# Value and output projections of a hybrid decoder layer: the 64-token tile with its low parts stacked beside its high parts

## The reference

```python
cb, cc, ch, q, k, v, g, a_lr, ga, gb = jnp.split(xn @ w_in, splits, axis=-1)   # xn = rmsnorm(x)
y_a = (cb * z) @ w_conv_out                     # z = short_conv(cc * ch)
o, S = gla(q, k, v, log_a, gla_state)           # gated linear attention, 4 heads
y_b = (rmsnorm(o) * silu(g)) @ w_gla_out
m = sigmoid(ga) * y_a + sigmoid(gb) * y_b
h = x + m @ w_o
h = h + hmoe(rmsnorm(h))                        # 32 experts, top-1 group, top-2 experts
y = rmsnorm(h)
```

## Time and profile before

| | us |
|---|---|
| median of 3 runs | 922.8 |
| lowest, highest | 921.0, 928.88 |
| the profiled execution | 922.86 |
| its span, from the first to the last instruction | 920.7 |

### The profile page before, as it was taken

One profiled execution on the slowest core, in us unless ns is written; L12 is line 12 of the kernel. 1 busy time (PEld: TensorE's weight loads), 2 busy tenths in 40 slices (PEclk: granted clock), 3 DMA queues, 4 the chain that ended last, 5 costly groups with the idle time before them and its releaser, 6 DMA issues.

```text
span 920.7 us, 12589 instructions
## 1 busy us (share of the span) xinstructions
PE 795.8 (86%) x5330; PEld 645.3 (70%) x5330; DVE 293.6 (32%) x507; ACT 237.6 (26%) x347; POOL 79.2 (9%) x121
## 2 busy tenths in 40 slices
PE   3899979999999999999999989965899788788740
PEld 3899979999988899999989989962333333233210
DVE  5420340566435362111464533243100000000007
ACT  5422432254411124422231211220221111111102
POOL 3000000001012210000000000111011100100003
PEclk9799989999999999999999989975999989988975
DMA  7412121111325642122215173179899999999726
GB/s 200 142 46 91 55 83 46 46 47 46 115 93 167 199 137 93 53 86 92 92 46 195 46 265 125 43 287 383 334 412 410 409 410 409 408 407 407 307 101 226
DMA packets 82147, 173.99 MB, mean 189 GB/s; under 512 B 10946, under 2 KB 49346, under 8 KB 81524
## 3 DMA queue, kind: packets, MB, share of 16 engines
q1 hardware_dynamic: 75108, 155.22, 46.1%
q0 software_dynamic: 6992, 18.10, 5.3%
HBM read 162.77 MB, written 17.86 MB: 196 GB/s over the span
## 4 chain that ended last, share of the span: by engine, by line
PE 74%; DMA 12%; DVE 5%; SPq 4%; ACT 3%; issue 2%; POOL 1%; POOLq 0%; ACTq 0%; DVEq 0%
PE ps L1535 52%; PE ps L1826 9%; DMA wgu<-w_up 9%; SPq L396 3%; PE ps L1843 3%; PE ps L1625 1%; DMA xin<-x_sample 1%; PE ps L1818 1%; PE ps L1683 1%; DMA xg<-moe_rows,slots 1%; PE ps L1672 1%; PE ps L1764 1%; PE ps L1639 1%; PE ps L1637 1%; PE ps L1636 1%
## 5 line engine op out<-in xcount | busy, mean ns | idle before, releaser
L1535 PE MATMUL ps<-xh,wh 128*128 128x288 f32 x832 | 181.6, 300 | 3.9 <-ACT hist L792 2.0
L1535 PE MATMUL ps<-xh,wl 128*128 128x288 f32 x832 | 179.4, 297 | 0.0
L1535 PE MATMUL ps<-xl,wh 128*128 128x288 f32 x832 | 179.2, 297 | 0.0
L1826 PE MATMUL ps<-wgu,gx 128*64 128x512 f32 x512 | 130.4, 668 | 27.5 <-DMA wgu<-w_up 26.4
L999 DVE TENSOR_TENSOR wl<-raw,wh 128x2048 fp32r<-128x2048 f32 x36 | 82.5, 2292 | 201.8 <-ACT wh L701 201.7
L1535 PEld LDWEIGHTS ps<-xh,wh 128*128 128x128 f32 x832 | 135.1, 190 | 7.7 <-issue 5.2
L1535 PEld LDWEIGHTS ps<-xh,wl 128*128 128x128 f32 x832 | 135.2, 190 | 0.0
L1535 PEld LDWEIGHTS ps<-xl,wh 128*128 128x128 f32 x832 | 134.9, 190 | 0.0
L1826 PEld LDWEIGHTS ps<-wgu,gx 128*64 128x64 f32 x512 | 44.1, 153 | 112.3 <-issue 110.8
L701 ACT CAST wh<-raw 128x2048 fp32r<-128x2048 f32 x36 | 68.6, 1905 | 61.0 <-PE ps L1535 59.6
L1479 DVE TENSOR_TENSOR hm<-si,ps 128x256 f32<-128x256 f32 x16 | 6.7, 421 | 227.7 <-ACT si L934 227.7
(11 more groups left out here) (296 smaller groups left out, 945.6 us busy)
## 6 DMA issues: line engine op xcount, KB each, us to landing
wgu<-w_gate SPq DMA_DIRECT2D x32, 1024.0 KB, 14.5
wgu<-w_up SPq DMA_DIRECT2D x32, 1024.0 KB, 20.3
wd<-w_down SPq DMA_DIRECT2D x32, 1024.0 KB, 20.2
raw<-w_in SPq DMA_DIRECT2D x26, 1024.0 KB, 5.3
raw<-w_gla_out SPq DMA_DIRECT2D x4, 1024.0 KB, 5.1
raw<-w_o SPq DMA_DIRECT2D x4, 1024.0 KB, 5.4
y<-moe_results SPq DMA_DIRECT2D x4, 1024.0 KB, 7.9
xin<-x_prompt SPq DMA_DIRECT2D x4, 512.0 KB, 6.5
```

Source lines behind the costliest of these rows:

```text
L1535: last.append(mm(out, left(a, k), right(b, k, o), start=k == 0 and n == 0, stop=k == k_tiles - 1 and n == 2))
L1826: ins = mm(ps[half * B:(half + 1) * B, bank, :].rearrange("t (n c) -> t n c", n=2), x[:, k, half * B:(half + 1) * B], w[half][:, :, :].rea ...
```

## The change

For the 64-token tile alone, the three passes become two. The 64 unused columns T to TP of `xh` and `mh` now hold the low parts of the 64 tokens. The stationary operand `[high | low]` (128 columns) is multiplied with `wh`: rows 0 to 63 of the PSUM region get high x high, rows 64 to 127 low x high. The second pass multiplies the 64 high columns with `wl` and adds to rows 0 to 63. So there are 16 matmuls in the place of 24, and the two halves of the region are added behind.

```diff
             def token_unit(p, u, t, x, ks=range(KD)):
                 w = (tiles(wh[p], KD), tiles(wl[p], KD))
+                if t == NPT:
+                    for k in ks:
+                        mm(ps[:, 2 * u, 0:256], x[0][:, k, SEQ:TP], w[0][:, k, :], start=k == 0, stop=False,
+                           skip_group_check=True)
+                        ins = mm(ps[0:ND, 2 * u, 0:256], x[0][:, k, SEQ:T], w[1][:, k, :], start=False, stop=k == KD - 1,
+                                 skip_group_check=True)
+                    return ins
```

```diff
             for i in range(NT):
                 rms(i, i, i + 1, D)
+            pool.wait_ge(unit_free[1], N_G // 2)
+            pool.tensor_tensor(v[0:ND, NPT, :], v[0:ND, NPT, :], vlo[:, :], ALU.add).then_inc(vd_ready, 1)
...
-                    copy(v[:, t, k * 256:(k + 1) * 256], ps[:, 2 * u, 0:256]).then_inc(unit_free[u], 1)
+                    if t == NPT:
+                        c(copy(v[0:ND, t, cols], ps[0:ND, 2 * u, 0:256]))
+                        copy(vlo[:, cols], ps[ND:P, 2 * u, 0:256]).then_inc(unit_free[u], 1)
...
-                    tt(hv, hv, ps[:, 2 * u, 0:256], ALU.add).then_inc(h_ready, 1)
+                    if t == NPT:
+                        hv = h[0:ND, t, k * 256:(k + 1) * 256]
+                        c(tt(hv, hv, ps[0:ND, 2 * u, 0:256], ALU.add))
+                        c.sync()
+                        tt(hv, hv, ps[ND:P, 2 * u, 0:256], ALU.add).then_inc(h_ready, 1)
```

```diff
-                tt(xl[:, :, i * P:(i + 1) * P], ps[...], xh[...], ALU.subtract).then_inc(xt_free, 1)
+                n = ND if i == NPT else P
+                if i == NPT:
+                    c(tt(xh[:, :, T:TP], x, high, ALU.subtract))
+                tt(xl[:, :, i * P:i * P + n], x, high, ALU.subtract).then_inc(xt_free, 1)
...
-            c(dve.memset(mh[:, :, T:TP].bitcast(F32), 0.0))
-            c(dve.memset(ml[:, :, T:TP].bitcast(F32), 0.0))
-            c.sync()
...
                         dve.wait_ge(m_hi, k * 2 + (u + 1))
+                        tt(mh[:, one, T:TP].rearrange("p a t -> p (a t)"), tmp[u][:, SEQ:T],
+                           mh[:, one, SEQ:T].rearrange("p a t -> p (a t)").bitcast(F32), ALU.subtract)
                         tt(ml[:, one, 0:T]..., ALU.subtract).then_inc(m_ready, 1)
```

More of the change, by code:

```diff
@@ L196, in build @@
         mnt = sb("mnt", [P, T])
+        vlo = sb("vlo", [ND, D], at=zone_q - 4 * D)
         m_tile = sb("m_tile", [P, H, P], at=s1)
@@ L328, in build @@
         st_store, km_ready, dkv_full, st_ready = (sem(n) for n in ("st_store", "km_ready", "dkv_full", "st_ready"))
-        pair_const = sem("pair_const")
+        vd_ready = sem("vd_ready")
         cc_ready, z_mul, z_hi, z_ready, cs_ready, cs_full, cso_ready = (
@@ L712, in high_of_x @@
                 b = TB + 2 * (i % 2)
-                copy(xh[:, :, i * P:(i + 1) * P], ps[:, b:b + 2, :].rearrange("p a (c t) -> p (a c) t", t=P)
+                n = ND if i == NPT else P
+                copy(xh[:, :, i * P:i * P + n], ps[:, b:b + 2, :].rearrange("p a (c t) -> p (a c) t", t=P)[:, :, 0:n]
                      ).then_inc(xh_ready, 1)
@@ L786, in _ @@
                     wait_unit(act, k + G_V, k, t, NT, U_V)
-                    copy(v[:, t, k * 256:(k + 1) * 256], ps[:, 2 * u, 0:256]).then_inc(unit_free[u], 1)
+                    cols = slice(k * 256, (k + 1) * 256)
+                    if t == NPT:
+                        c(copy(v[0:ND, t, cols], ps[0:ND, 2 * u, 0:256]))
+                        copy(vlo[:, cols], ps[ND:P, 2 * u, 0:256]).then_inc(unit_free[u], 1)
+                    else:
+                        copy(v[:, t, cols], ps[:, 2 * u, 0:256]).then_inc(unit_free[u], 1)
                 high(k % 2, (G_V + k) // 2 + 1)
@@ L1007, in low_of_x @@
                 b = TB + 2 * (i % 2)
-                tt(xl[:, :, i * P:(i + 1) * P], ps[:, b:b + 2, :].rearrange("p a (c t) -> p (a c) t", t=P),
-                   xh[:, :, i * P:(i + 1) * P].bitcast(F32), ALU.subtract).then_inc(xt_free, 1)
+                n = ND if i == NPT else P
+                x = ps[:, b:b + 2, :].rearrange("p a (c t) -> p (a c) t", t=P)[:, :, 0:n]
+                high = xh[:, :, i * P:i * P + n].bitcast(F32)
+                if i == NPT:
+                    c(tt(xh[:, :, T:TP], x, high, ALU.subtract))
+                tt(xl[:, :, i * P:i * P + n], x, high, ALU.subtract).then_inc(xt_free, 1)
             for i in range(NT):
@@ L1341, in _ @@
                     wait_unit(dve, g, k, t, NT, U_WO)
-                    hv = h[:, t, k * 256:(k + 1) * 256]
-                    tt(hv, hv, ps[:, 2 * u, 0:256], ALU.add).then_inc(h_ready, 1)
+                    if t == NPT:
[3 more added lines that the diff above has]
+                        tt(hv, hv, ps[ND:P, 2 * u, 0:256], ALU.add).then_inc(h_ready, 1)
+                    else:
+                        hv = h[:, t, k * 256:(k + 1) * 256]
+                        tt(hv, hv, ps[:, 2 * u, 0:256], ALU.add).then_inc(h_ready, 1)
                     dve.wait_ge(h_ready, NT * k + t + 1)
@@ L1658, in decode_within @@
                 pe.wait_ge(on_ready, NPT + 1)
+                pe.wait_ge(vd_ready, 1)
                 for hd in range(H):
```

## The result

| | us |
|---|---|
| before, median of 20 runs | 922.41 (920.68 to 928.91) |
| changed, median of 20 runs | 918.04 (915.01 to 920.35) |
| ratio, 95% interval | 0.9939 (0.9924 to 0.9954) |
| profiled execution before, its span | 922.86, 920.7 |
| profiled execution changed, its span | 915.66, 913.4 |

The change makes the kernel faster by 0.6%, 5.6 us with 4.2 to 7.0 us as bounds (0.0061, 0.0046 and 0.0076 of 922.41). 14 us slower had been forecast. It is the rival "no pause" that came true: it gave 916.4 us. The ratio lies near that of the means (917.9 and 923.7 us) and not of the medians, which are 4.4 us apart: seven of the 20 runs before took 925 us or more, and none of the changed kernel's took more than 920.4.

A forecast was written before the change was run, and what follows sets the result against it. PE, busy 86% of the span, was taken to bound the kernel through the projections' matmuls. Matmuls +12.8 us and the other steps +1.25 us made +14.0 us on 922.9, 936.9 us, say 937; 8 in 10 for 929 to 948 us.

The forecast's parts named there:

- no pause: Rival, projections' new units: 128*64 products follow 128*128 ones freely, 7.7 us off, 1.25 us added, 916.4 us; chance 0.06.
- What the remaining 16 cost: Eight rewritten projection units: pauses and open loads make a pair cost 0.57 us against 0.36 us; +12.8 us in all.
- half pace: Rival, second pass: the 64-column float32r product's columns take twice as long, +6.8 us, 944 us; chance 0.05.
- What is removed: Both projections: each of eight units loses 8 of 24 matmuls at 0.121 us, 7.7 us off by count.
- Two copies for one: Value projection, ACT: the second copy is on the path at groups 5 and 7, +0.5 us.
- POOL's addition: After the value projection, 64x1024: takes 1.8 to 3.6 us, covered by POOL's idle time, adds nothing.
- Low part of x: Fifth tile, ahead of the first projection: one 1.22 us instruction becomes two of 0.68 us, +0.1 us.
- Low part into `mh`: Output projection: seven of eight hide under PE's units, the last lies between ACT's `mh` and `ml`, +0.2 us.
- Two additions to `h`: Output projection, DVE: hidden in three groups, at the end ahead of ACT's square of the last tile, +0.45 us.
- The shift arrives at the end: Expert stage and all behind it: moves one for one by what the projections gain or lose.
- Half a pause: Rival, new units: 0.10 us pause stays but loads come forward under it, pair 0.42 us, 927.6 us; chance 0.08.
- The clock falls in the new units: Rival: TensorE's clock falls, 2.4 us each; four of eight units give 946.5 us, all 956 us; chance 0.11.

The follow-up runs named there:

- The first experiment: Changed kernel plus ten unused series of 256-column matmuls ahead of the attention output's first transpose, mixing float32r or float32, 128 or 64 columns or rows: 938.46 us, one run.

## Why the prediction was wrong

**The step that failed: "What the remaining 16 cost".** A change to 128*64 and back was put at 0.10 us behind the columns and an open load; a pair at 0.57 us, a unit at 4.6 us, the eight at +12.8 us. A pair takes 0.234 us and a unit 1.87 us. The pause exists and its size was right (0.09 us behind the columns, 0.10 and 0.05 us of open load), but for another kind of product: every row that I used for columns was float32 (L1650 and L1672 multiply float32 tiles), was a change of rows, and the products of the new unit are float32r. The first experiment puts both side by side: float32 pays it (4.5 us for 3.5 us), float32r does not (1.8 and 1.8 us). I had seen that the trace before has no float32r product in 128*64, and priced that gap for its columns alone (half pace); I did not carry it over to the pause. And the earlier trace rows was the sign: the label 128*64 with no pause. I put it down to the transposes and gave the rival that it supports 0.06.

The Trainium skill's sentence ("TensorEngine Tiling (Array Packing)", Key Properties: changing the tiling mode drains TensorE) agrees with the float32 series (0.09 us behind the columns, 0.17 us a change) and with the rows of float32r (0.2 us a change). For the columns of float32r the label changes 128 times in this kernel and nothing drains. Either the sentence doesn't hold for that type or, as theory A has it, the part of the array doesn't change there whatever the label says; the series with one label and two types speaks for the second. Why the transposes of the earlier trace rows don't pause no run shows.

**The rest of the sum.**

- *What is removed: 7.7 us.* Right in kind. A unit took 2.88 us (24 x 0.120) and takes 1.87 us (16 x 0.117), 1.01 us less and not 0.96: 8.1 us in all.
- *Two copies for one*: +0.5 us was forecast, +0.8 us it is by ACT's rows with and without the copy (twice 0.40), and +1.0 us by PE's waits before and after (5.3 to 5.8 and 2.0 to 2.5 us).
- *POOL's addition*: nothing, right. It took 2.3 us where 1.8 to 3.6 us were the bounds, and ended long before the next norm factor:

```profile
155.58 2.34 POOL L579 TENSOR_TENSOR v<-v,vlo 64x1024 f32<-64x1024 f32 x1 [140.63 <-ACT vlo L794]
180.67 0.20 POOL L572 TENSOR_SCALAR ms<-ss 128x4 f32<-128x4 f32 x1 [22.75 <-ACT v L816]
```

- *Low part of x*: two pieces of 0.68 us start 0.60 us apart and end 1.28 us behind the first's start, in the place of one of 1.22 us. +0.1 us is right.
- *Low part into `mh`*: 0.2 us forecast. The instruction takes 225 ns, and PE's wait for the last `ml` grows from 3.5 to 3.8 us: +0.3 us.
- *Two additions to `h`*: +0.45 us forecast. They follow each other, and ACT's square starts behind the second:

```profile
596.73 0.41 DVE L1356 TENSOR_TENSOR h<-h,ps 64x256 f32<-64x256 f32 x1 [2.20 <-PE ps L1571]
597.18 0.42 DVE L1358 TENSOR_TENSOR h<-h,ps 64x256 f32<-64x256 f32 x1
597.63 1.06 ACT L906 ACTIVATE junk<-h 64x1024 f32<-64x1024 f32 x1 [4.73 <-DVE h L1358]
```

0.90 us from the first addition to the square, where one took 0.46 us (604.53 to 604.99): +0.44 us, right.

- *The shift arrives at the end*: right, by 7.4 us at the router against 7.2 us at the end.

With these sizes the sum is -8.1 + 0.8 + 0.1 + 0.3 + 0.45 = -6.45 us (-6.25 with the copies by PE's waits), inside the measured 4.2 to 7.0 us, and beside the profile's 7.2 us, in which the clock has its part: 0.9 us at the return from the stall and over 1 us behind `hist` in favour of the changed kernel, about 1.3 us at 476 against it.

**The rivals.** "No pause" came true with its price (916.4 us; the ratio gives 916.8 us, the profile 915.66). "Half a pause" and "half pace" are out: pairs start 0.234 us apart. "The clock falls in the new units" is out: in the first profile no stretch at the lower level begins in one of them.

## What to carry to other kernels

A pause read from a trace belongs to the instructions that showed it: ask of each row whether type, rows and columns are those of the new instruction, and if one differs, keep the case without the pause as a real one. When a tile has half the tokens, the other half of the stationary columns is free in float32r: stacking the low parts there saves a pass for the price of one more eviction. Put that second eviction behind whatever the next stage waits for: here it shortened PE's waits by 0.9 us, which the time alone could not show.

## What the runs showed of the hardware that was not expected

- float32r products with 128 and with 64 stationary columns alternate at 0.117 us a piece of 256 columns, without a pause; a 64-column product costs nearly as much (0.114 us) as one of 128 (0.119 to 0.120 us).
- float32 products with the same shapes pause at each change: 16 records in 4.5 us in the place of 3.5 us. Two of them with 64 columns each, in the two halves of the array, run at the same time: 16 records in 2.0 us.
- float32r products with 128 and with 64 *rows* do pause: 16 in 4.8 us in the place of 1.8 us, 0.2 us a change.
- Products of one shape and label (64 columns), one float32r and one float32, pause between each other; of 128 columns they don't.
- An ACT copy from PSUM behind another from the same region costs 0.40 us of ACT's chain, where a copy ahead of a weight block's cast costs 0.27 us. Before the change two copies from two regions took 0.63 us together, 0.26 us from start to start (133.14); whether the one region or the 64 partitions make the difference no run shows.
